# Attention scores of four heads at once by row groups of the matmul array, and products with the values every fourth step

## The reference, cut to what matters

```python
# q: 96 per head (64 plain + 32 rotary);  k: 64 plain per head, and 32 rotary that all heads share
q = _rmsnorm(concat(q_nope, q_rope), q_norm_g)     # over the 96 of each head
k = _rmsnorm(concat(k_nope, broadcast(k_rope)), k_norm_g)
# image rows (rope is not None): the 32 rotary elements are turned by position
s = einsum('bqhd,bkhd->bhqk', q, k) * 96 ** -0.5
o = einsum('bhqk,bkhd->bqhd', softmax(s), v)
x = x + gate * (concat([fx, gx, o * silu(a)]) @ w_out)
```

## Time and profile before

| what | value |
|---|---|
| median of 3 runs | 878.61 us (878.52 to 880.6) |
| the profiled execution | 880.03 us, of which span 878.2 us |
| PE busy | 858.1 us (98%) |
| VectorE busy | 637.8 us (73%) |
| ScalarE busy | 448.5 us (51%) |
| granted TensorE clock | 0.996 of full speed |

### The profile page before, as it was taken

One profiled execution on the slowest core, in us unless ns is written; L12 is line 12 of the kernel. 1 busy time (PEld: TensorE's weight loads), 2 busy tenths in 40 slices (PEclk: granted clock), 3 DMA queues, 4 the chain that ended last, 5 costly groups with the idle time before them and its releaser, 6 DMA issues.

```text
span 878.2 us, 13397 instructions
## 1 busy us (share of the span) xinstructions
PE 858.1 (98%) x5364; PEld 710.6 (81%) x5364; DVE 637.8 (73%) x1256; ACT 448.5 (51%) x763; POOL 23.5 (3%) x19
## 2 busy tenths in 40 slices
PE   8999999999999999999999999999999999999996
PEld 4678578776686888778998888989999888888885
DVE  4534879675656789966699999978588765565665
ACT  3353545554633564655443544556554765555552
POOL 0000000000000000000003113000000000000000
PEclk9999999999999999999999999999999999999999
DMA  9785543202173135213665665532366365645541
GB/s 351 306 308 190 216 186 114 85 1 77 44 263 110 35 103 170 84 45 112 197 203 167 193 194 179 155 120 72 108 205 207 118 207 190 207 167 202 186 174 48
DMA packets 40717, 138.25 MB, mean 157 GB/s; under 512 B 4432, under 2 KB 4560, under 8 KB 40400
## 3 DMA queue, kind: packets, MB, share of 16 engines
q1 hardware_dynamic: 40224, 134.41, 45.3%
q10 hardware_dynamic: 432, 3.00, 0.9%
HBM read 136.34 MB, written 1.05 MB: 156 GB/s over the span
## 4 chain that ended last, share of the span: by engine, by line
PE 65%; DVE 26%; ACT 4%; DMA 2%; issue 2%; SPq 0%; DVEq 0%; POOLq 0%; POOL 0%; ACTq 0%
DVE wlo L1507 9%; PE ps L412 9%; PE ps L987 6%; DVE AF L2025 6%; PE ps L413 4%; PE ps L367 3%; PE ps L749 3%; PE ps L368 3%; PE ps L372 3%; PE ps L384 2%; DMA AF<-wmod 2%; PE ps L487 2%; PE ps L772 2%; PE ps L395 2%; PE ps L385 2%; PE ps L386 2%
## 5 line engine op out<-in xcount | busy, mean ns | idle before, releaser
L1027 ACT ACTIVATE whi<-raw 128x1024 fp32r<-128x1024 f32 (+3 forms) x213 | 211.5, 1002 | 99.3 <-DMA raw<-wpack 58.4
L1507 DVE TENSOR_TENSOR wlo<-raw,whi 128x1024 fp32r<-128x1024 f32 (+3 forms) x213 | 240.9, 1154 | 27.4 <-ACT whi L1027 27.2
L367 PE MATMUL ps<-hx,whi 128*128 128x256 f32 (+1 forms) x384 | 115.4, 301 | 0.5 <-ACT AF L1383 0.3
L412 PE MATMUL ps<-hx,whi 128*128 128x512 f32 x320 | 113.9, 398 | 0.0
L368 PE MATMUL ps<-hx,whi 128*128 128x256 f32 (+1 forms) x384 | 112.0, 292 | 0.0
L372 PE MATMUL ps<-hx,wlo 128*128 128x256 f32 (+1 forms) x332 | 96.9, 292 | 0.0
L413 PE MATMUL ps<-hx,wlo 128*128 128x256 f32 x320 | 89.8, 281 | 0.0
L367 PEld LDWEIGHTS ps<-hx,whi 128*128 128x128 f32 x384 | 73.4, 191 | 4.2 <-issue 2.3
L368 PEld LDWEIGHTS ps<-hx,whi 128*128 128x128 f32 x384 | 73.4, 191 | 2.0 <-issue 0.7
L457 PE MATMUL ps<-whi,hx 128*128 128x512 f32 (+1 forms) x192 | 71.8, 374 | 0.9 <-DVE lat L1643 0.9
L412 PEld LDWEIGHTS ps<-hx,whi 128*128 128x128 f32 x320 | 60.1, 188 | 14.6
(11 more groups left out here) (319 smaller groups left out, 1677.9 us busy)
## 6 DMA issues: line engine op xcount, KB each, us to landing
raw<-wpack SPq DMA_DIRECT2D x181, 512.0 KB, 4.1
AF<-wmod SPq DMA_DIRECT2D x48, 512.0 KB, 6.6
raw<-wpack SPq DMA_DIRECT2D x24, 256.0 KB, 3.1
raw<-wpack SPq DMA_DIRECT2D x6, 384.0 KB, 3.0
XT<-xin SPq DMA_DIRECT2D x4, 512.0 KB, 6.7
raw<-wpack SPq DMA_DIRECT2D x4, 432.0 KB, 5.5
cst<-cpack ACTq DMA_DIRECT2D x1, 1349.0 KB, 8.6
AF<-l2rows ACTq DMA_DIRECT2D x1, 1024.0 KB, 7.5
```

The lines of the kernel that those rows point to most:

```text
L367: e.matmul(o, wh[:, b], xh(k), start=j == 0, stop=False, skip_group_check=True)
L412: e.matmul(ps.ap(key, 512).rearrange("p (s n) -> p s n", s=2), wh[:, b], K.hx[:, :, k, 0:256], start=k == 0, stop=False, skip_group_check= ...
L1027: e.activation(W.hi(i), W.raw(i), ACT.Copy).then_inc(*HI.up(j))
L1507: e.tensor_tensor(W.lo(i), W.raw(i), W.hi(i), ALU.subtract).then_inc(*LO.up(j))
```

## The change

Queries and keys are stored in two parts. The plain part has two heads under each other (`g.Qn`, `g.Kn`: rows 0 to 63 and 64 to 127), the rotary part four heads (`g.Qr`, `g.Kr`: 32 rows each). A tile is turned with 4 + 2 transposes of 128x128 in place of 8 of 128x96. `scores(i)` is called at every fourth step for four heads, in PSUM banks 0 to 3, which are waited for all together: four products of 32 rows, then four of 64 rows that add to them. All else shares banks 4 to 7 (`ps.low = 4`) until the last item.

The keys' rotary part is turned once for all heads (`key_turns`) and only scaled per head. Its sum of squares comes from four small ScalarE operations a layer. `q_proj(1)` moves from step 8 to step 3, the turning of the image keys to step 7, of the image queries to steps 11 and 15. `values` for four heads come in a row at every step with i % 4 == 3, and now behind `BESIDE` and `BEGUN`. On ScalarE `exps(i)` goes ahead of `pt(i - 3)` except at every fourth step. A finished gate is taken in the same step where i % 4 == 3 (`soon`).

```diff
+        g.krx, g.krt = area(128), area(128)
+        g.Qn = area(1024).rearrange("p (y j n) -> p y j n", y=2, j=4)
+        g.Qr = area(512).rearrange("p (y j n) -> p y j n", y=2, j=2)
...
+        g.Kn = area(4 * TT).rearrange("p (j n) -> p j n", j=4)
+        g.Kr = area(2 * TT).rearrange("p (j n) -> p j n", j=2)
...
+def soon(l, i):
+
+    return i % 4 == 3 and i in BESIDE[l] and BESIDE[l][i][2] and BESIDE[l][i][0] != "gws"
...
-            for h0 in (0, 4):
-                key = (l, nm + "T", p, y, h0)
+            for part, c, n in (("n", 0, 4), ("r", 512, 2)):
+                key = (l, nm + "T", p, y, part)
                 pe.wait_ge(*ps.take(key))
-                for j in range(4):
-                    i = e.transpose(ps.ap(key, P, j * P, slice(0, 96)), g.X[x][:, y * 768 + (h0 + j) * 96:y * 768 + (h0 + j + 1) * 96], C("ident"))
+                for j in range(n):
+                    a = y * 768 + c + P * j
+                    i = e.transpose(ps.ap(key, P, j * P), g.X[x][:, a:a + P], C("ident"))
                 i.then_inc(*M.up(key))
...
         def scores(i):
+
             t, h = items[i]
             n = (2 if t < 2 else 4) * P
-            key = (l, "s", i)
-            pe.wait_ge(*K.heads_done(l, "q", t // 2, t % 2), *K.heads_done(l, "k", 0), *(K.heads_done(l, "k", 1) if t >= 2 else []), *ps.take(key))
-            e.matmul(ps.ap(key, n), g.Q[0:96, t % 2, h, :], g.K[0:96, h, 0:n], start=True, stop=True, skip_group_check=True).then_inc(*M.up(key))
+            pe.wait_ge(*K.heads_done(l, "q", t // 2, t % 2), *K.heads_done(l, "k", 0), *(K.heads_done(l, "k", 1) if t >= 2 else []))
+            pe.wait_ge(*(x for j in range(4) for x in ps.take((l, "s", i + j), at=j)))
+            for j in range(4):
+                r = slice(32 * j, 32 * j + 32)
+                e.matmul(ps.ap((l, "s", i + j), n), g.Qr[r, t % 2, h // 4, :], g.Kr[r, h // 4, 0:n], start=True, stop=False, skip_group_check=True)
+            for j in range(4):
+                r = slice(64 * (j % 2), 64 * (j % 2) + 64)
+                e.matmul(ps.ap((l, "s", i + j), n), g.Qn[r, t % 2, (h + j) // 2, :], g.Kn[r, (h + j) // 2, 0:n],
+                         start=False, stop=True, skip_group_check=True).then_inc(*M.up((l, "s", i + j)))
...
-            if i < ni:
+            ps.low = 4 if i < ni - 1 else 0
+            if i < ni and i % 4 == 0:
                 scores(i)
             if 0 <= i - 3 < ni:
                 turned(i - 3)
-            if l == 0 and i == 8:
-                q_proj(1)
-            if l == 0 and i == 6:
-                heads_T("k", 1, 0, 0)
-            if l == 0 and i == 7:
-                heads_T("k", 1, 0, 1)
-            if l == 0 and i == 15:
-                heads_T("q", 1, 0, 0)
-            if l == 0 and i == 17:
-                heads_T("q", 1, 0, 1)
-            if i >= 5 and i % 2:
-                values(i - 5)
             if i in BESIDE[l]:
                 nm, m, a = BESIDE[l][i]
                 if nm == "gws":
@@ -806,9 +816,19 @@
                     lin_rest(half, xh, xl, N, ht, ht)
                     if (nm, m) == ("gu", 1):
                         M.mark(("hread", l))
+            if l == 0 and i == 3:
+                q_proj(1)
             if i in BEGUN[l]:
                 m = BEGUN[l][i]
                 begun.append(lin_first((l, "wout", m), "w_out", l, (P * m, P), 4, xh, xl, N, mt))
+            if i >= 7 and i % 4 == 3:
+                values(i - 7)
+                values(i - 5)
+            if l == 0 and i == 7:
+                for y in range(2):
+                    heads_T("k", 1, 0, y)
+            if l == 0 and i in (11, 15):
+                heads_T("q", 1, 1, i // 15)
...
+        def kr_squares(t):
+            ac.wait_ge(A.now())
+            e.activation(g.krt[:, 64:96], g.kr[:, t * 32:(t + 1) * 32], ACT.Square, accum_out=g.stat[:, 8 + t:9 + t]).then_inc(*A.up((l, "krss", t)))
...
+            if i < ni and i % 4:
+                exps(i)
             if 0 <= i - 3 < ni:
                 pt(i - 3)
-            if i < ni:
+            if i < ni and i % 4 == 0:
                 exps(i)
-            if i - 1 in BESIDE[l] and (BESIDE[l][i - 1][2] or BESIDE[l][i - 1][0] == "gws"):
+            if i - 1 in BESIDE[l] and not soon(l, i - 1) and (BESIDE[l][i - 1][2] or BESIDE[l][i - 1][0] == "gws"):
                 beside(*BESIDE[l][i - 1][:2])
             if l == 0 and i == 0:
-                squares("k", 1, 0, 2, V[l, "krb", 1], V[l, "gvr"])
-            if l == 0 and i == 6:
-                heads_T("k", 1, 0, 0)
+                squares("k", 1, 0, 2, V[l, "gvr"])
+            if soon(l, i):
+                beside(*BESIDE[l][i][:2])
             if l == 0 and i == 7:
-                heads_T("k", 1, 0, 1)
-            if l == 0 and i == 8:
-                highs((l, "uq", 1, 0))
-                q_take(1, 0, M[l, "kT", 1, 1, 4])
-            if l == 0 and i == 9:
-                squares("q", 1, 0, 2, V[l, "rope", "k", 1])
-            if l == 0 and i == 15:
-                heads_T("q", 1, 0, 0, M[l, "s", 7])
-            if l == 0 and i == 17:
-                heads_T("q", 1, 0, 1, M[l, "s", 15])
+                for y in range(2):
+                    heads_T("k", 1, 0, y)
...
+        def key_turns():
+
+            kr, kx = (x[:, 0:128].rearrange("p (t n) -> p t n", t=4) for x in (g.kr, g.krx))
+            part = g.krt[:, 0:64].rearrange("p (t a b n) -> p t a b n", t=2, a=2, b=2)
+            x4 = kr[:, 2:4, :].rearrange("p t (a b n) -> p t a b n", a=2, b=2)
+            tb, g32 = tab[1]
+            gs = tb[:, 64:128].rearrange("p (t a b n) -> p t a b n", t=2, a=2, b=2)
+            dv.wait_ge(A[l, "gv", 3], V[l, "tab"])
+            e.tensor_tensor(kx[:, 2:4, :], kr[:, 2:4, :], tb[:, 0:64].rearrange("p (t n) -> p t n", t=2), ALU.mult).then_inc(*V.up())
+            for hf in range(2):
+                e.tensor_tensor(part[:, :, :, hf, :], x4[:, :, :, 1 - hf, :], gs[:, :, :, hf, :], ALU.mult).then_inc(*V.up())
+            dv.wait_ge(V.now())
+            e.tensor_tensor(kx[:, 2:4, :], kx[:, 2:4, :], g.krt[:, 0:64].rearrange("p (t n) -> p t n", t=2), ALU.add).then_inc(*V.up())
+            dv.wait_ge(A[l, "krT"] if l else None)
+            e.tensor_tensor(kx[:, 0:2, :], kr[:, 0:2, :], g32.unsqueeze(1).broadcast_to([P, 2, 32]), ALU.mult).then_inc(*V.up((l, "krx")))
+            dv.wait_ge(*(A[l, "krss", t] for t in range(4)))
+            e.tensor_scalar(g.stat[:, 8:12], g.stat[:, 8:12], 1.0 / 96, EPS, ALU.mult, ALU.add).then_inc(*V.up((l, "kre")))
+
+        def v_take(p):
...
+            a, b = ys[0], ys[-1] + 1
+            s8 = ss.rearrange("p (y h) -> p y h", y=2)[:, a:b, :].unsqueeze(3)
+            Xn, Xr = g.Xn[x][:, a:b], g.Xr[x][:, a:b]
+            dv.wait_ge(V.now(), A[l, "hsq", nm, p])
+            e.tensor_tensor(Xn, Xn, s8.broadcast_to([P, b - a, 8, 64]), ALU.mult).then_inc(*V.up())
+            src = g.krx.rearrange("p (t n) -> p t n", t=4)[:, 2 * p + a:2 * p + b, :].unsqueeze(2).broadcast_to([P, b - a, 8, 32]) if nm == "k" else Xr
+            e.tensor_tensor(Xr, src, s8.broadcast_to([P, b - a, 8, 32]), ALU.mult).then_inc(*V.up())
```

More of the change, by code:

```diff
@@ L121, in begin @@
     def begin(self):
-        self.clock, self.holder, self.held, self.age = 0, [None] * 8, set(), [0] * 8
+        self.clock, self.holder, self.held, self.age, self.low = 0, [None] * 8, set(), [0] * 8, 0
     def take(self, key, n=1, hold=False, at=None):
-        free = [i for i in (range(9 - n) if at is None else (at,)) if not any(j in self.held for j in range(i, i + n))]
+        free = [i for i in (range(self.low, 9 - n) if at is None else (at,)) if not any(j in self.held for j in range(i, i + n))]
         if not free:
@@ L242, in geometry @@
         g.Vf = area(4 * 512).rearrange("p (t n) -> p t n", t=4)
-        assert max(o, end) <= K.NAF, max(o, end)
+        end = max(o, end)
+        assert end <= K.NAF, end
         g.late = K.AF[:, end - 8192:end]
         g.X = [tq, K.wk[:, 0:1536], tq2]
+        parts = [x.rearrange("p (y c) -> p y c", y=2) if x is not None else None for x in g.X]
+        g.Xn = [x[:, :, 0:512].rearrange("p y (h d) -> p y h d", h=8) if x is not None else None for x in parts]
+        g.Xr = [x[:, :, 512:768].rearrange("p y (h d) -> p y h d", h=8) if x is not None else None for x in parts]
         g.scr = [K.AF[:, ko - 3072:ko - 1536], K.AF[:, ko - 1536:ko], scr2]
@@ L1202, in gv_squares @@
             e.activation(g.gsq[:, 0:256 * len(tiles)], g.gv[:, tiles[0] * 256:1024], ACT.Square).then_inc(*A.up((l, "gvsq")))
+        for t in range(4):
+            kr_squares(t)
         if l == 0:
@@ L1208, in layer @@
         if l == 0:
-            squares("k", 0, 0, 0, V[l, "krb", 0])
+            squares("k", 0, 0, 0)
             q_take(0, 1, M[l, "cqsum"])
@@ L1226, in layer @@
             highs((l, "fgate", 1), 0)
-            squares("k", 0, 0, 0, V[l, "krb", 0])
-            squares("k", 1, 2, 2, V[l, "krb", 1], V[l, "gvr"])
+            squares("k", 0, 0, 0)
```

(41 more changed lines are left out.)

113 lines of the change are left out of this document (47 added, 66 removed).

## The result

The changed kernel takes 883.21 us (median of 7 runs, 881.56 to 886.38) against 879.6 us of the kernel before on the same chips (7 runs, 878.52 to 881.64): a ratio of 1.0042, 95% interval 1.0023 to 1.006, so slower by 3.6 us. The forecast was 877.5, with 872.5 to 883.5.

The account below looks back on a forecast made before the run. TensorE (PE) was taken to set the pace. Its work -9.7 us, old waits -4.3 and new waits +12.9 gave -1.1 us: 877.5 against the median of 878.6, range 872.5 to 883.5.

Parts of the forecast that it names:

- PE's own work: TensorE time in both attentions: cheaper scores, fewer switches, merged values and fewer transposes together save 9.7 us.
- C: Rival: the four 32-row groups of the scores run in pairs, not all at once; +8.6, 886.1 us; chance 0.10.
- Old waits: TensorE's seven existing stalls in the two attentions all go: -4.3 us.
- New waits: Waits that grouped scores, late values and fewer free banks bring to TensorE in both layers: +12.9 us.
- layer 0, group of step 24, up to step 28's scores: TensorE idles until VectorE's row of work, including spatial gating, lets the fourth head's exponent finish: 3.8 us.
- layer 1, step 15: TensorE waits for the probabilities of item 12 behind VectorE's spatial gating: +2.6 us.
- the two ends: End of each layer: gate and output after the last values are no longer hidden under a projection; 1.5 us twice, +3.0.
- wait of some 4 us for the exponent: Sign to look for in TensorE's waits at layer 0's step 28, on the successor of line L1265.
- A: The forecast itself: most of TensorE's gain goes into waits; 877.5 us, own range 875 to 880.5; chance 0.48.
- D: Rival: the four banks hold TensorE at every group, eight other groups waiting 0.7 more each; +5.6, 883.1 us; chance 0.12.
- E: Rival: no effect, as the second block starts earlier but waits for its weights; 878.6 us; chance 0.06.
- B: Rival: the waits stay small and the row-group switch is free; 871.6 us at best, 873 likely; chance 0.24.

Follow-up runs that it names:

- e_sp0: Changed kernel with layer 0's spatial product behind step 23's values and its four VectorE operations at the end of step 23: 881.0 us, ratio 1.0016.
- f_sp1: Changed kernel with layer 1's spatial gating operations on VectorE at step 11, ahead of the output gate, not at step 12: 881.9 us, ratio 1.0024.
- g_gv: Changed kernel with layer 1's gate value factors and their products on VectorE at step 7, not at steps 2, 4 and 6: 881.6 us, ratio 1.0025.
- h_all: Changed kernel with e_sp0, f_sp1, g_gv, last-step values ahead of the begun projection, and layer 0's second image query tile rotated at step 13: 874.4 us.
- d_merged: Kernel before with only the values of four heads merged, behind the work beside; scores one head at a time: 879.6 us, ratio 1.0003.
- i_moves: Control: kernel before with the same three moves of VectorE work as e_sp0, f_sp1 and g_gv: 879.3 us, ratio 0.9991.
- m_bank: h_all with the turned modulation row ahead of the first scores put into banks 4 to 7: 874.1 us, ratio 0.9927.
- a_again: The changed kernel run once more, unaltered, for a second trace: 883.3 us, ratio 1.0044.
- l_burst: d_merged with scores of 512 keys four at a time in banks 0 to 3, one 96-row product a head, changed ScalarE order: 899.2 us, ratio 1.022.

## Why the prediction was wrong, step by step

**PE's own work: right in kind, forecast -9.7, measured about -12.6.** Values in a row 1.9 and turning 0.109 a transpose are as forecast. Scores are cheaper, 2.99 and not 3.18 eight times (-1.5), 1.71 and not 1.89 four times (-0.7). C, four row groups in pairs, is refuted by the 1.28 us between the two sizes. The 12.6 is not measured by itself: it is what remains of the differences by stretch when waits and half clock are taken out, and it is the same in both traces. The scores account for 2.2 us of the 2.9 between forecast and measurement; the rest is open.

**Old waits: right.** The stalls of the earlier trace rows are gone from their places except two, counted below among the new: the one for the last query copy in layer 1, still 0.6, and the bank of `q_proj(1)`, 0.5 before and 0.7 now.

**New waits: the step that failed.** It was summed to 12.9; by distances between starts the two traces of the changed kernel have 17.7 and 18.7. Term by term:

| place | forecast | measured |
|---|---|---|
| layer 0, group of step 24, up to step 28's scores | 3.8 | 4.2 |
| layer 1, step 15 | 2.6 | 2.7, and 1.0 more in one trace |
| layer 1, step 4 | 1.5 | 1.7 |
| the two ends | 3.0 | 3.3 |
| layer 0, step 7 | 0.9 | 0.6 |
| `q_proj(1)` at step 3 | 0.5 | 1.1 |
| ahead of the first scores (a bank, a load) | 0 | 1.2 |
| layer 0, step 13, a bank | 0 | 1.3 |
| layer 1, before the first scores | 0 | 0.8 |
| others | 0.6 | 1.0 |

(The rounded column adds to 17.9.) The places and the large sizes were right: VectorE's row of work set the next group, and moving three pieces of it gave time back (e_sp0, f_sp1, g_gv). The group behind step 24 starts 12.96 us after it (212.60 to 225.56), and the forecast had 12.8. But the wait of some 4 us for the exponent that was named as a sign didn't come: 0.4 us of it are left, since PE had already waited 1.3 us for the spatial product's banks and 1.7 for a copy.

Two things were missed. The many small waits were put at 0.6, and 4.3 came. And a bank of the four left for all else can be late, not only at step 7: at step 13 of layer 0 PE waits 1.1 us for one that `out_gate` (L1965) gives back only behind the rotation (`rope`) and the copy of queries on VectorE; in h_all, with that rotation two steps later, the wait is gone. The waits on L1800 in both layers (1.3 and 0.6 us) are of this kind too.

**What no step had: the clock.** Every trace with scores in fours and the waits has one to three stretches at the half clock in the attentions, except f_sp1; no trace of the kernel before, d_merged, i_moves, h_all or m_bank has any there. All 13 lie in or behind a wait of 1.5 us or more; waits of 1.6 to 1.8 us in other places passed without one. The two that were measured cost 1.65 and 1.7 us.

Added up over the stretches behind the Fourier product, the two traces of the changed kernel are 0.8 and 1.8 us longer than the one of before without the half clock, and 2.5 and 3.5 with it; the medians differ by 3.6. So a third to a half of the loss in these traces is waits beyond what PE gained, and the rest the half clock.

All executions together fit this: the mean granted clock is 0.9942 over the 12 of the changed kernel and 0.9963 over the 23 of the kernel before beside a_again. The difference of 0.0021 is worth 1.9 us of 881 at most, about half of the 3.6. Without a trace it can't be told where in an execution that half clock lies. The executions of h_all have a mean clock of 0.9945 too, with none in the attentions of its trace; behind the Fourier product that trace is 6.8 us shorter than the one of before, and the median only 5.1.

That the waits bring the half clock is suggested by its absence wherever they are small. It isn't shown: no run changes the clock alone, and stretches of it ahead of the Fourier product are found in the kernel before too (at 82 us).

The errors had opposite signs. PE's work was 2.9 us lighter than forecast, the new waits were 4.8 to 5.8 us longer, and the half clock added 1.7: from -1.1 that gives 2.5 to 3.5.

**A against D.** A's mechanism held, at A's places, with PE's gain going into waits, and yet the time is that of D, 883.1, by coincidence. D would have wanted a wait for banks 0 to 3 at all groups: those at steps 4 to 24 of layer 0 and 8 and 12 of layer 1, eight of twelve, start without one. The Trainium skill's rule behind D ("TensorEngine Tiling (Array Packing)", Gotcha 1: PSUM Pressure) says that row tiling increases the pressure on PSUM. The trace agrees at step 13 (1.1 us) and in the waits on L1800, where what is short is the banks for the other work. l_burst takes the same four banks without row tiles and waits for a bank as well (6.3 us). E is out, since the second block follows at its own length (469.0 to 469.1), in h_all and m_bank too, where it starts earlier behind the Fourier product. B didn't happen: its waits did not stay small. That h_all and m_bank, at 874.1 to 874.4, come near its 873 takes five moves that B didn't have, and confirms nothing of it.

## What to carry to other kernels

Work put in lockstep (four heads, four banks, one start) moves the bound to the engine that must finish the group: before it is timed, that engine's work should be moved to where it waits for the group to arrive. Price waits on TensorE like these, 1.5 us and more in a busy stretch, with the half clock that may follow them. When banks are set aside for a group, count who else needs them, and look at the order in which each helping engine takes its pieces. And try a grouping together with its partners: merged values were worth nothing alone, scores in fours lost 3.2 us in one layer, both with a rearranged VectorE and covered ends gained 5.

## What the runs showed of the hardware

Four products of 32 rows with 512 columns in float32 went side by side at no loss that grows with the columns: 8 MATMUL in 1.07 us (200.30 to 201.37), where one product of 96 rows takes 0.86. With 256 columns it is 0.64 against 0.43: in both cases 0.21 more than one product, as a switch would cost. By the whole 1.07, four tiles are 3.2 times as fast as one after the other (4 x 0.86). The Trainium skill has 3.07 times ("TensorE: Matmul & The Clock Gate", Part 3, Measured speedup vs the span model). An estimate by it is 4 x 0.86 / 3.07 = 1.12, near the 1.07 here, if its figure holds the switch too.

The second new thing is the half clock beside waits in the middle of a busy stretch: PE was busy before and after, waited 1.5 to 4.1 us, and got 0.50 for 3.4 or 6.8 us, in some executions and not in others of the same kernel. In two of the 13 cases the clock fell before the wait was over.
